# The front stage of a hybrid decoder layer: u's products 512 columns wide, the Toeplitz blocks put together in DRAM, y in pairs of groups, and the scan's inputs between the z products

## The reference, cut to what matters

```python
x = _rmsnorm(h, norm1_g)
proj = x @ w_in                         # 1024 -> 512 (u) + 1792 (zr)
u, zr = proj[..., :D_SSM], proj[..., D_SSM:]
# S5: 32 groups of 16 channels, each with a 64-wide complex diagonal state
bu = einsum('blgc,gpc->blgp', ug, bb)   # bb: discretised input matrix
h_t = ab * h_{t-1} + bu_t               # ab = exp(lam * dt), complex
y = Re(einsum(h, c)) + d_skip * u
y = gelu(y);  y = y * sigmoid(y @ w_glu + b_glu)
```

## Time and profile before

| what | us |
|---|---|
| median of three runs | 3764.75 |
| the profiled execution | 3759.42 |
| its span, first to last instruction | 3757.6 |
| of it the front stage, to its last store | 899.6 |
| start to the first u product | 98.0 |
| u of the first half | 98.4 |
| the first b product to the end of z | 128 |
| end of z to the first GLU product | 175.4 |

### The profile page before, as it was taken

One profiled execution on the slowest core, in us unless ns is written; L12 is line 12 of the kernel. 1 busy time (PEld: TensorE's weight loads), 2 busy tenths in 40 slices (PEclk: granted clock), 3 DMA queues, 4 the chain that ended last, 5 costly groups with the idle time before them and its releaser, 6 DMA issues.

```text
span 3757.6 us, 78861 instructions
## 1 busy us (share of the span) xinstructions
PE 3461.2 (92%) x33808; PEld 3288.5 (88%) x33808; DVE 2014.4 (54%) x3597; ACT 1175.3 (31%) x2314; POOL 556.8 (15%) x499
## 2 busy tenths in 40 slices
PE   5998989896988999985999999999999999999998
PEld 5988989474888888875999999999999999999998
DVE  6322119612666666642655555666555566655565
ACT  3122231112444444432322222542222254222234
POOL 2121112002333333312101000310100031000001
PEclk9999999577999999986999999999999999999999
DMA  3122112202011111014422222532332253232223
GB/s 112 32 79 86 56 32 71 29 1 84 26 28 28 38 28 28 16 32 130 124 83 68 72 68 69 156 99 83 99 103 68 68 157 99 68 99 72 68 77 117
DMA packets 409810, 267.91 MB, mean 71 GB/s; under 512 B 36976, under 2 KB 399984, under 8 KB 409456
## 3 DMA queue, kind: packets, MB, share of 16 engines
q1 hardware_dynamic: 409488, 263.07, 23.6%
HBM read 228.60 MB, written 34.30 MB: 70 GB/s over the span
## 4 chain that ended last, share of the span: by engine, by line
PE 48%; DVE 3%; issue 1%; ACT 1%; POOL 0%; SPq 0%; DMA 0%; POOLq 0%; DVEq 0%; ACTq 0%
PE oe_pg L699 13%; PE oe_pd L727 13%; PE oe_pv L699 13%; PE oe_pd L747 4%; PE oe_pg L760 4%; DVE oe_w_lo L509 1%; PE oe_pv L767 1%; DVE oe_rms L540 0%; ACT oe_w_hi L360 0%; DVE oe_x L525 0%; DMA oe_raw<-in_w_ple 0%; POOL oe_ys_lo L308 0%; POOL oe_acc L326 0%; DVE oe_h L516 0%; PE oe_pn L688 0%
## 5 line engine op out<-in xcount | busy, mean ns | idle before, releaser
L509 DVE TENSOR_TENSOR oe_w_lo<-oe_raw,oe_w_hi 128x1024 fp32r<-128x1024 f32 (+1 forms) x294 | 381.0, 1306 | 112.9 <-ACT oe_w_hi L360 86.6
L516 DVE TENSOR_TENSOR oe_h<-oe_pd,oe_h 128x352 f32<-128x352 f32 x576 | 292.5, 522 | 190.3 <-PE oe_pd L727 139.9
L727 PE MATMUL oe_pd<-oe_f_hi,oe_w_hi 128*128 128x352 f32 x1056 | 342.8, 325 | 8.3 <-DVE oe_h L516 8.3
L2326 PE MATMUL fr_bk<-fr_xs,fr_ring 128*128 128x352 f32 (+2 forms) x2016 | 340.1, 330 | 10.3 <-DVE fr_xs L2190 10.3
L699 PE MATMUL oe_pg<-oe_xs_hi,oe_w_hi 128*128 128x352 f32 x1056 | 342.1, 324 | 6.3 <-DVE oe_xs_lo L530 6.3
L2326 PEld LDWEIGHTS fr_bk<-fr_xs,fr_ring 128*128 128x128 f32 x2016 | 332.4, 193 | 15.6 <-issue 15.0
L360 ACT CAST oe_w_hi<-oe_raw 128x1024 fp32r<-128x1024 f32 (+1 forms) x294 | 312.4, 1073 | 93.7 <-DMA oe_raw<-in_w_out 39.9
L699 PE MATMUL oe_pg<-oe_xs_lo,oe_w_hi 128*128 128x352 f32 x1056 | 340.4, 322 | 0.0
L727 PE MATMUL oe_pd<-oe_f_lo,oe_w_hi 128*128 128x352 f32 x1056 | 340.3, 322 | 0.0
L699 PE MATMUL oe_pg<-oe_xs_hi,oe_w_lo 128*128 128x352 f32 x1056 | 340.3, 322 | 0.0
L727 PE MATMUL oe_pd<-oe_f_hi,oe_w_lo 128*128 128x352 f32 x1056 | 340.2, 322 | 0.0
(11 more groups left out here) (380 smaller groups left out, 7443.9 us busy)
## 6 DMA issues: line engine op xcount, KB each, us to landing
oe_raw<-in_w_gate SPq DMA_DIRECT2D x66, 512.0 KB, 4.0
oe_raw<-in_w_val SPq DMA_DIRECT2D x66, 512.0 KB, 4.0
oe_raw<-in_w_down SPq DMA_DIRECT2D x66, 512.0 KB, 3.7
oe_raw<-in_w_out SPq DMA_DIRECT2D x48, 512.0 KB, 3.8
oe_raw<-in_w_pg SPq DMA_DIRECT2D x48, 512.0 KB, 3.8
fr_raw<-in_w_in SPq DMA_DIRECT2D x72, 256.0 KB, 3.0
rw_Z<-scratch_zr SPq DMA_DIRECT2D x15, 903.0 KB, 5.4
oe_h<-in_xT SPq DMA_DIRECT2D x6, 1408.0 KB, 11.5
```

What stands on the lines that cost most here:

```text
L509: dve.tensor_tensor(w_view(kind, lo), w_view(kind, raw[i % 2]), w_view(kind, hi).bitcast(F32), ALU.subtract).then_inc(w_lo, 1)
L516: dve.tensor_tensor(hm, pd[sums[key] % 3][:, 0:TW], hm, ALU.add).then_inc(h_ready, 1)
L727: mm = pe.matmul(pd[turn % 3][:, 0:TW], l, r, start=(q == 0 and j == 0), stop=(q == G - 1 and j == 2))
L2326: mm = pe.matmul(out, lhsT, rhs, start=(k == 0 and p == 0), stop=(k == KD - 1 and p == 2))
```

## The change

- **u**: one unit makes all 512 columns, with the four weight blocks of u in the four slots at once; 17 units in place of 34. The lead of z products ahead of u is four blocks in the first half and two in the second (`LEAD`).
- **Order**: the turns U follow u among the z products in both halves, four at a time; the b units come four at a time behind each of eight z products.
- **Tm**: a DRAM scratch is set to zero from a zero tile, the eight shifted pieces are copied DRAM to DRAM, and one DMA loads `Tm` when slots 0 and 1 are free, five z products before the end of z. POOL's memset goes.
- **y**: two banks at once; for a pair of an even and an odd group both Tm products, then the CA products in turns between the two halves of the rows.
- **Qp**: the powers of the scan are stored with the step innermost.
- **Start**: ACT's and DVE's parameter work moves from the kernel's start to behind the eviction of z (2, 3), the last one ahead of u. The squares, roots and loads of the x tiles 3 to 5 come earlier.

The diff, cut to its core:

```diff
+LEAD = (4, 2)
 RING = [(h, kind, m) for h in range(2)
-        for kind, ms in (("z", range(4)), ("u", range(KU)), ("z", range(4, ZT))) for m in ms]
+        for kind, ms in (("z", range(LEAD[h])), ("u", range(KU)), ("z", range(LEAD[h], ZT))) for m in ms]
...
+            for m in range(LEAD[h]):
                 yield ("z", n, m)
                 if n == 5:
+                    for f in range(4 * m, 4 * m + 4):
+                        yield ("R", f)
+        if h == 0:
+            yield ("u", 2, 0)
+        for s in range(L):
+            yield ("u", h, s)
         turn = 0
+        for m in range(LEAD[h], 10 if h == 0 else ZT):
             for n in ns:
                 yield ("z", n, m)
+                if h and turn < 2 * NJ and m > LEAD[h]:
+                    for i in range(turn, turn + 4):
+                        yield ("b", i // NJ, i % NJ)
+                    turn += 4
+                if m == LEAD[h]:
+                    for f in range(4 * (n % 3), min(4 * (n % 3) + 4, 8)):
+                        yield ("U", h, f)
...
-        Qp = e.sb("Qp", [P, 2, BI + 1, NJ])
+        Qp = e.sb("Qp", [P, 2, NJ, BI + 1])
...
+                    if unit == ("z", 0, 5):
+                        sp.wait_ge(const_ready, 3)
+                        sp.dma_start(tm_mem, nought[:].unsqueeze(1).to_broadcast([P, NG_, P])).then_inc(tm_put, 16)
+                    if unit == ("z", 0, 7):
                         x_tile(3)
-                    if unit == ("z", 2, 10):
+                    if unit == ("z", 1, 11):
                         x_tile(4)
-                    if unit == ("z", 3, 0):
+                    if unit == ("z", 2, 11):
                         x_tile(5)
...
+                    if unit == ("z", 0, 12):
+                        sp.wait_ge(tm_put, 16)
+                        sp.wait_ge(ks_stored, 16)
+                        for s in range(L):
+                            sp.dma_start(tm_mem[s * GC:(s + 1) * GC, :, s * GC:P], ks_mem[:, :, 0:P - s * GC]).then_inc(tm_put, 16)
+                    if unit == ("z", 4, 12):
+                        sp.wait_ge(tm_put, 16 * (L + 1))
+                        wait_last_use(sp, len(RING) - 4)
+                        wait_last_use(sp, len(RING) - 3)
+                        sp.dma_start(Tm, tm_mem).then_inc(tm_in, 16)
                 store(*before)
-                sp.wait_ge(tm_zero, 1)
-                sp.wait_ge(ks_stored, 16)
-                for s in range(L):
-                    sp.dma_start(Tm[s * GC:(s + 1) * GC, :, s * GC:P], ks_mem[:, :, 0:P - s * GC]).then_inc(tm_in, 16)
...
+                        if (n, m) == (2, 3):
+                            parameters()
...
-                def u_unit(out, lot, s_, c):
+                def u_unit(out, lot, s_):
+                    pe.wait_ge(w_lo_ready, 2 * RING_AT[int(lot == 1), "u", KU - 1] + 2)
-                        lot3 = three([xs[:, a, k, tokens] for a in range(2)], [ring[:, slot:slot + 2, a, k, :] for a in range(2)])
+                        lot3 = three([xs[:, a, k, tokens] for a in range(2)], [ring[:, :, a, k, :] for a in range(2)])
-                            mm = pe.matmul(out[0:n, 0:2 * P], lhsT, rhs, start=(k == 0 and p == 0), stop=(k == KD - 1 and p == 2))
+                            mm = pe.matmul(out[0:n, :], lhsT, rhs, start=(k == 0 and p == 0), stop=(k == KD - 1 and p == 2))
...
-                        if (n, m) == (0, 13):
+                        if (n, m) == (0, 12):
                             mean_square(3)
-                        if (n, m) == (2, 11):
+                        if (n, m) == (1, 13):
                             mean_square(4)
-                        if (n, m) == (3, 3):
+                        if (n, m) == (2, 13):
                             mean_square(5)
...
+                    for q in range(0, UG, 2):
                         i = li_ * UG + q
                         if i >= 4:
+                            pe.wait_ge(y_out, i - 2)
+                        for n4 in range(4):
+                            part_ = slice(n4 * P, (n4 + 1) * P)
+                            x = [range(NG_)[groups(q + h)][n4] for h in range(2)]
+                            for h in range(2):
+                                pe.matmul(bk[(i + h) % 4][0:n, part_], U[:, x[h], b0:b0 + n], Tm[:, x[h], :], start=True, stop=False)
                             for a in range(2):
+                                for h in range(2):
+                                    j, hs = x[h] // 2, slice(NS * h, NS * h + NS)
+                                    state = h0[hs, a, j, :] if lot == 2 else H[hs, a, j, b0:b0 + n]
+                                    mm = pe.matmul(bk[(i + h) % 4][0:n, part_], state, CA[hs, a, j, 1:, :], start=False, stop=(a == 1))
```

More of the change, by code:

```diff
@@ L1776, in front @@
             side_at[u] = len(side_at)
-            used = [RING_AT[int(u[1] == 1), "u", 2 * u[3] + i] for i in range(2)] if u[0] == "u" else []
+            used = [RING_AT[int(u[1] == 1), "u", i] for i in range(KU)] if u[0] == "u" else []
         for i in used:
@@ L1811, in front @@
         smp = CAf[0:TS, 2048:2048 + DSSM]
-        u_rows = [Hf[:, 1 - h, 0:NG_ * P] for h in range(2)]
+        u_rows = [Hf[:, 1 - lot % 2 if lot < 2 else 0, 0:NG_ * P] for lot in range(3)]
         R = U[:, :, P:2 * P].rearrange("p (x j) (s c) -> p x j s c", x=2, c=GC)
@@ L1822, in front @@
         ks_mem = nc.dram_tensor("scratch_ks", (GC, NG_, P), F32, kind="Internal").ap()
+        tm_mem = nc.dram_tensor("scratch_tm", (P, NG_, P), F32, kind="Internal").ap()
+        nought = e.sb("nought", [P, P])
         bk = [e.ps(f"bk{i}", [P, 512]) for i in range(8)]
@@ L1896, in x_tile @@
                 def x_tile(n):
+                    if n == 3:
+                        sp.wait_ge(side_mm, side_done("U", 2, 7))
                     if n >= 2:
@@ L1979, in _ @@
                 pool.memset(ones[:], 1.0 / D).then_inc(const_ready, 1)
+                pool.memset(nought[:], 0.0).then_inc(const_ready, 1)
                 pool.memset(eps[:], RMS_EPS).then_inc(const_ready, 1)
@@ L2036, in side_evict @@
                     if kind == "u":
-                        _, lot, s, c = unit
+                        _, lot, s = unit
                         if lot == 2:
-                            dst, src = smp[:, 256 * c:256 * c + 256], src[0:TS, 0:256]
+                            dst, src = smp, src[0:TS]
                         else:
@@ L2190, in norm @@
                         dve.tensor_tensor(xs[:, 1, ks, cols(n)], q[:, ks], xs[:, 0, ks, cols(n)].bitcast(F32), ALU.subtract).then_inc(x_lo, 1)
+                dve.wait_ge(g_in, 16)
+                for n in range(3):
+                    norm(n)
                 dve.wait_ge(par_in, 16 * NPAR)
@@ L2199, in _ @@
                 dve.sem_inc(arg_ready, 1)
-                dve.wait_ge(g_in, 16)
-                for n in range(3):
-                    norm(n)
                 dve.wait_ge(sc_ready, 3)
@@ L2274, in _ @@
                 link(dve.memset(H[:, :, :, 0:1], 0.0))
-                a8 = [bcast(Qp[:, x, 1, :], BI) for x in range(2)]
+                a8 = [bcast(Qp[:, x, :, 1], BI) for x in range(2)]
                 for i in range(1, BI):
@@ L2281, in _ @@
                     link(dve.tensor_copy(G[:, x, :, 1:], ends[:, x, :, 0:BI - 1]))
-                a128 = [Qp[:, x, BI, :].unsqueeze(2) for x in range(2)]
+                a128 = [Qp[:, x, :, BI:BI + 1] for x in range(2)]
                 for b in range(1, BI):
@@ L2285, in _ @@
                 for r in range(BI):
-                    add_product(H[:, :, :, 1 + r * BI:1 + (r + 1) * BI], [Qp[:, x, 1:, :].rearrange("p i j -> p j i") for x in range(2)],
+                    add_product(H[:, :, :, 1 + r * BI:1 + (r + 1) * BI], [Qp[:, x, :, 1:] for x in range(2)],
                                 G[:, :, :, r:r + 1].to_broadcast([P, 2, NJ, BI]), tmp)
@@ L2290, in _ @@
                 dve.wait_ge(h0_in, 32)
-                add_product(HS[:], [bcast(Qp[:, x, 1, :], NBS) for x in range(2)], h0[:], tmp[:, :, :, :, 0:NBS])
+                add_product(HS[:], [bcast(Qp[:, x, :, 1], NBS) for x in range(2)], h0[:], tmp[:, :, :, :, 0:NBS])
                 for i in range(2):
```

110 lines of the change are left out of this document (39 added, 71 removed).

## The result

The changed kernel takes 3607.68 us (median of four runs, 3600.65 to 3610.10) against 3762.48 of the kernel before (four runs, 3758.66 to 3765.74): a ratio of 0.9586, 95% interval 0.9568 to 0.9603. Forecast were 3602, in a range of 3570 to 3645. The profiled execution took 3610.1, its span is 3608.3.

A forecast was written before the change was run, and what follows sets the result against it. PE's path through the front, up to a barrier, was taken as the bound: -74 us to the scan's start and -83.6 after it make -157 of 3759.4, so 3602 us, range 3570 to 3645.

The forecast's parts named there:

- u: u's prompt matmuls: 768 become 384 of 512 columns, step staying 242 ns, set by the strided load; -93.2 us.
- The start: Kernel start: with ACT's parameter work moved away, the first square starts at 9.4, not 13.64; -4.2 us.
- The gaps at u: Around u: moved parameter work, evictions, casts, subtractions and late fourth turns U make PE wait; +24.4 us.
- Waits that go: Ahead of the scan: PE's waits for the sample's DMA, sums of squares and turns between u's parts shrink; -21.1 us.
- The scan's start: DVE's scan: begins 74 us earlier, at about 475, after 20.5 us lost to z products and b's ahead of it.
- From there: Scan's start to GLU products: 203 us instead of 286.6, with the scan on the path before lot 0; -83.6 us.
- The sum: Start of the GLU products: -74 and -83.6 give -157 us, a total of 3602.
- both costlier cases: Total time: load and columns adding in u, 3646; pairs not side by side, 3634; range meant to include both.
- Load and columns add: Rival in u: a matmul costs load plus columns, so widening gives back less; 3646 us; chance 0.11.
- Pairs not side by side: Rival in y: CA products of the two halves do not run side by side; +32, 3634 us; chance 0.06.
- The slow clock through the z products: Rival in z: new gaps hold the clock at 1.2 GHz, 3.7 us more per product; up to 3868; chance 0.03.
- Lot 0 at full clock: Rival in y's first prompt lot: clock rises to 1.00, 3593 us; chance 0.75 together with the forecast.

The follow-up runs named there:

- the two in-line experiments: u's stationary operand read in line (128 tokens in a row, not every eighth): in the kernel before, 3673.66 us; in the changed kernel, 3593.05 us.
- parameters late: Changed kernel with ACT's parameter work behind the two casts of u's fourth block instead of ahead of them: 3602.24 us.
- b's in a row: Changed kernel with all 32 b units in a row behind one z product, instead of four behind each of eight: 3587.53 us.

## Why the prediction was right, step by step

- **u**, forecast -93.2: measured 98.4 to 55.7 and 93 to 48.9, -86.8. The mechanism is shown by the two in-line experiments, and undoing the width alone costs 81.4. The size missed by 6.4: the first unit took 8.3 us, not 5.3, at a PEclk of 0.64 behind the gap, the second half ran at 0.97, and a step is 245 to 247, not 242. "Clock lost in old gaps and in new ones I take as equal" was the step that failed for the larger part of it; the smaller part is the step at 512 columns, 3 to 5 ns above the 242 that the load was to set at either width. The Trainium skill's estimate of 107 ns for a load ("TensorE: Matmul & The Clock Gate", section "LDWEIGHTS (loading the stationary operand)") is not contradicted for an operand in line, where the step of 121 is an upper bound; it misses the strided operand's 240 by more than half.
- **The start**, -4.2: the first square starts at 9.28 for 13.64, -4.4.
- **The gaps at u**, +24.4: 8.2 for 8.6 in front of the first u, 1.0 for 1, 3.8 for 4.1 twice behind. The waits of the fourth turns came, but shorter: 2.5 and 1.3 where I gave them 3.3 twice (second row below). 20.5 in sum, so the forecast had 3.9 too much.
- **Waits that go**, -21.1. The sums of squares were the miss, 16.4 left, not 11.7. Their row (the first here, 196 to 424 us; the second counts from 157) and SP's timeline (start, us, what) show the cause:

```profile
PE fr_bk L2325 <- DVE fr_H L2189: 16.4, 3, 11.7
PE fr_bk L2358 <- ACT fr_U L2066: 3.8, 2, 2.5
```

```profile
288.42 17.10 SPq L1916 DMA_DIRECT2D scratch_zr<-fr_zout  x5
310.33 1.64 SPq L1909 DMA_DIRECT2D fr_raw<-in_w_in  x2
312.01 0.60 SPq L1900 DMA_DIRECT2D fr_H<-in_xT  x1
```

  The norm ahead frees x tile 5's buffer at 305.7, but the load is issued at 312.0, behind five stores and the two halves of a weight block in SP's queue. I had looked at the buffer and not at the queue.
- **The scan's start**, 475: it is 480.5, 5.5 late. The errors above come to 7.0 (u 6.4 and the sums of squares 4.7 later, the gaps 3.9 and the start 0.2 earlier). Most of the rest lies in waits that the sum left out: K, which waited 2.8 us before, no longer does, and R's turns wait 1.5, which they did not.
- **From there**, +203: it is 197.8. z takes 92.4 (92.6), `h_ready` 1 comes at +128.5 (130), lot 1 takes 20.6 (20.5), the rest to the GLU 9.4 (9.0). Two sizes were off by the clock: the sample lot took 17.2 at full clock where I gave it 30 at half, and lot 0 33.0 for 36.8, its clock rising near its end. The sample lot was at full clock with y's groups one after another too, and at 0.91 with the wait for `Tm` back, so it is more likely the missing wait than the pairs that kept its clock up. The time so gained is worth nothing, since the scan is on the path, as the prediction said. Lot 0's 3.8 and `h_ready`'s 1.5 are what remained.
- **The sum.** -156.9 at the GLU against -157: that it is so near is luck, two errors of 5 met. The execution itself lost 149.3 and came out at 3610, not 3602, since the unchanged stages behind the front took 7.6 more; they vary by 11 between the kernels here. So "a microsecond taken off its end is one off the total" holds to within that only. The range, too, was to take in both costlier cases; the dearer one, 3646, lies 1 above its end.
- **The rivals.** Load and columns add: refuted in u directly. Pairs not side by side: refuted by CA's two products a step. The slow clock through the z products: it was 1.00 behind the last b. Lot 0 at full clock: it came so in one experiment (`Tm` as before), which gained 6.2 at the GLU, and partly in others.

What stays open is lot 0's clock. With the same products in lot 0 its PEclk was 0.58 in the changed kernel and 0.66, 0.53 and 1.00 in three that differ only ahead of it (parameters late, b's in a row, `Tm` as before). The wait for the scan doesn't decide it: 0.53 was the kernel without that wait, and in the changed kernel the clock was at half by 592.5, among the sample's turns and 2.3 us before that wait began:

```profile
592.50:594.80 2.30, 2.30 (x23) 2.25 (x22) 2.20 (x4) 1.27 (x6) 0.00 (x0) 0.50 0.00 0
```

## What to carry to other kernels

Compare the weight loads' recorded time with that of a load of the same shape elsewhere in the trace: where it is longer, the operand's stride is the suspect, and an operand in line takes the cost away, or wider products most of it (19 ns of 121 a matmul were left at 512 columns). When a change speeds up several producers of one point, work out which comes last there afterwards: here a transfer that had cost 14.5 us cost nothing once the scan was last, and what the interleaved order cost the scan was then on the path. And a load that is issued in order is late by whatever stands ahead of it in its queue, not only by its buffer.

## What the runs showed of the hardware

- A weight load of 128 x 128 with its columns eight elements apart sets a step of 240 to 242 ns at 256 columns; in line it allows 121. At 512 columns the steps are 245 to 247 and 228. The recorded durations of the load are 331 to 339 strided and 188 to 192 ns in line.
- Products on the upper and the lower 64 rows run side by side whether they are issued in turns or two and two: with the order even, even, odd, odd the eight records still start in four twos, 13 to 15 ns apart, and the last of the even group, the fourth in the kernel's order, is one of the last two (both of these, and no other of the eight, raise the semaphore that each group's last product raises).
- In y at full clock every run of one shape (128-row or 64-row products) costs 0.2 us besides its 0.11 a step, so fewer changes between the shapes save time: shown by runs of two, four and sixteen steps.
